# ScalarE's gate function reads PSUM itself; its clamp becomes a minimum in VectorE's product

## What is computed

```python
gu = xb @ w_gu[e] + b_gu[e]                                # rows x 2048
x_glu = jnp.minimum(gu[:, :D_FF], SWIGLU_LIMIT)            # limit 7.0
x_lin = jnp.clip(gu[:, D_FF:], -SWIGLU_LIMIT, SWIGLU_LIMIT)
act = x_glu * jax.nn.sigmoid(SWIGLU_ALPHA * x_glu) * (x_lin + 1)   # alpha 1.702
return act @ w_down[e] + b_down[e]                         # rows x 1024
```

## Time and profile before

| | |
|---|---|
| time, 3 runs | 1763.78 us median (1761.51 to 1766.02) |
| profiled execution | 1762.76 us, of which the span is 1761.0 us |
| TensorE matmul | 1653.0 us busy, 94% of the span |
| TensorE weight load | 1301.0 us, 74% |
| VectorE | 1342.6 us, 76% |
| ScalarE | 1123.3 us, 64% |
| GpSimd | 643.0 us, 37% |
| HBM read | 476.44 MB |

### The profile page before, as it was taken

How to read it: one execution, slowest core, us unless ns; L and a number is a source line. 1 busy time by engine, 2 the same in 40 slices (tenths; PEclk the granted TensorE clock), 3 DMA queues, 4 the chain that set the end, 5 groups by cost and what they waited for, 6 DMA issues and landing times.

```text
span 1761.0 us, 22444 instructions
## 1 busy us (share of the span) xinstructions
PE 1653.0 (94%) x7739; PEld 1301.0 (74%) x7739; DVE 1342.6 (76%) x1184; ACT 1123.3 (64%) x1030; POOL 643.0 (37%) x480
## 2 busy tenths in 40 slices
PE   6999999999988889999999999999999999999993
PEld 5877767889866576877777777777777777777762
DVE  4444563426343569999999999999999999999992
ACT  4134555234324245777887888888878878888882
POOL 5002231000000026346455455456456456456442
PEclk9999999999999998999999999999999999999996
DMA  9221112424441137999999999999999999999993
GB/s 317 106 95 62 60 65 74 150 79 147 164 122 48 60 130 287 392 389 395 399 401 399 402 399 397 400 399 396 400 398 398 401 403 392 402 397 395 400 377 105
DMA packets 93730, 493.11 MB, mean 280 GB/s; under 512 B 10461, under 2 KB 10530, under 8 KB 44426
## 3 DMA queue, kind: packets, MB, share of 16 engines
q1 hardware_dynamic: 82368, 459.30, 65.6%
q0 software_dynamic: 9824, 28.05, 6.0%
q10 hardware_dynamic: 1482, 5.01, 0.7%
HBM read 476.44 MB, written 20.38 MB: 282 GB/s over the span
## 4 chain that ended last, share of the span: by engine, by line
PE 40%; DVE 25%; issue 16%; DMA 9%; ACT 9%; SPq 0%; POOL 0%; DVEq 0%; ACTq 0%; POOLq 0%
DVE wlo L1548 17%; PE ps L1825 7%; PE ps L1826 7%; PE ps L1827 7%; DMA raw<-in_w_down 7%; ACT whi L1114 5%; PE ps L2278 4%; DVE glu L1588 2%; PE ps L1948 2%; PE ps L1950 2%; PE ps L1952 2%; PE ps L2248 1%; PE ps L1975 1%; DMA raw<-in_w_gu 1%; DVE lin L1590 1%
## 5 line engine op out<-in xcount | busy, mean ns | idle before, releaser
L1548 DVE TENSOR_TENSOR wlo<-raw,whi 128x2048 fp32r<-128x2048 f32 x380 | 847.3, 2283 | 33.0 <-ACT whi L1114 32.4
L1114 ACT ACTIVATE whi<-raw 128x2048 fp32r<-128x2048 f32 x380 | 716.0, 1913 | 98.8 <-DMA raw<-in_w_gu 53.3
L700 POOL TENSOR_TENSOR mark<-ident 1x1 f32<-1x1 f32 x32 | 158.6, 4956 | 340.8 <-ACT ybuf L1156 222.0
L1274 DVE TENSOR_TENSOR wlo<-raw,whi 128x2048 fp32r<-128x2048 f32 x52 | 119.3, 2317 | 147.0 <-ACT whi L846 147.0
L701 POOL DMA_INDIRECT moe_rows<-ybuf,ycur x32 | 207.4, 6482 | 6.3 <-issue 6.3
L2278 PE MATMUL ps<-whi,xhi 128*128 128x512 f32 x544 | 151.6, 401 | 3.4 <-DVE xlo L1553 2.7
L2278 PE MATMUL ps<-wlo,xhi 128*128 128x512 f32 x544 | 146.5, 391 | 0.0
L2278 PE MATMUL ps<-whi,xlo 128*128 128x512 f32 x544 | 146.5, 391 | 0.0
L846 ACT ACTIVATE whi<-raw 128x2048 fp32r<-128x2048 f32 x52 | 98.1, 1917 | 71.7 <-DVE branch L1425 30.2
L2224 PE MATMUL ps<-whi,xhl 128*128 128x512 f32 x480 | 132.4, 397 | 9.3 <-DVE xhl L1558 9.2
L2224 PE MATMUL ps<-wlo,xhl 128*128 128x512 f32 x480 | 128.6, 390 | 0.0
(11 more groups left out here) (383 smaller groups left out, 3044.3 us busy)
## 6 DMA issues: line engine op xcount, KB each, us to landing
raw<-in_w_gu SPq DMA_DIRECT2D x256, 1024.0 KB, 9.9
raw<-in_w_down SPq DMA_DIRECT2D x128, 1024.0 KB, 8.3
raw<-in_w_in SPq DMA_DIRECT2D x14, 1024.0 KB, 10.0
raw<-in_w_gate SPq DMA_DIRECT2D x8, 1024.0 KB, 5.0
raw<-in_w_xkv SPq DMA_DIRECT2D x8, 1024.0 KB, 5.0
raw<-in_w_attn_up SPq DMA_DIRECT2D x4, 1024.0 KB, 4.8
raw<-in_w_out SPq DMA_DIRECT2D x4, 1024.0 KB, 5.2
raw<-in_w_xq SPq DMA_DIRECT2D x4, 1024.0 KB, 6.8
```

The lines of the kernel that those rows point to most:

```text
L700: g.tensor_tensor(mark[:, 0:1], ident[0:1, 0:1], ident[0:1, 1:2], ALU.add)
L1114: s.activation(his[m % DEPTH], raws[m % RAWS], ACT.Copy).then_inc(hi_done, 1)
L1274: v_.tensor_tensor(wlo[:, u % RING, :], raw[:, u % RING, :], whi[:, u % RING, :].bitcast(F32), ALU.subtract).then_inc(lo_done, 1)
L1548: v_.tensor_tensor(los[m % DEPTH], raws[m % RAWS], his[m % DEPTH].bitcast(F32), ALU.subtract).then_inc(lo_done, 1)
```

## The change

The `min` at 7 in front of the gate function goes (VectorE, L1588, one instruction an expert, 32 in all). ScalarE reads PSUM banks 0 and 1 itself and waits for TensorE's `unit_used` (or, for a light expert, `gu_shifted`) in place of `glu_ready`. The gate function rises beyond 0, so the clamp is taken behind it: VectorE's product becomes `hid = min(sig, GELU_LIMIT) * lin`, with the function's value at 7. The `+ 1` of the linear half moves into its bias (one more VectorE instruction on `braw`, once), and its clip goes from [-7, 7] to [-6, 8]. TensorE's bias product, which opens the banks anew, now waits for `sig_ready` as well.

```diff
+GELU_LIMIT = LIMIT / (1.0 + math.exp(-ALPHA * LIMIT))
...
-        glu = at("glu", 108, [CAP, D])
-        sig = glu
+        sig = at("sig", 108, [CAP, D])
...
-            def gate(i1, n=CAP):
-
-                act.wait_ge(glu_ready, i1)
-                s.activation(sig[0:n, :], glu[0:n, :], ACT.Gelu_apprx_sigmoid).then_inc(sig_ready, 1)
+            def gate(i1, used_value, n=CAP):
+
+                act.wait_ge(unit_used, used_value)
+                gate_rows(i1, n)
+
+            def gate_light(i1, lights):
+
+                act.wait_ge(gu_shifted, lights)
+                gate_rows(i1, SLOTS_L)
+
+            def gate_rows(i1, n):
+                s.activation(in_turn(sig[0:n, :]), every_second(ps[0:n, 0:2, :]), ACT.Gelu_apprx_sigmoid
+                             ).then_inc(sig_ready, 1)
...
             dve.wait_ge(braw_in, 96)
+            link(v_.tensor_scalar(braw[:, D:2 * D], braw[:, D:2 * D], 1.0, None, ALU.add))
             link(v_.tensor_copy(btmp[:, :], braw[:, :]))
...
             def gate_rows(i1, n, between=None):
-                v_.tensor_scalar(in_turn(glu[0:n, :]), every_second(ps[0:n, 0:2, :]), LIMIT, None, ALU.min
-                                 ).then_inc(glu_ready, 1)
-                v_.tensor_scalar(in_turn(lin[0:n, :]), every_second(ps[0:n, 2:4, :]), LIMIT, -LIMIT, ALU.min,
+                v_.tensor_scalar(in_turn(lin[0:n, :]), every_second(ps[0:n, 2:4, :]), LIMIT + 1.0, 1.0 - LIMIT, ALU.min,
                                  ALU.max).then_inc(gu_read, 1)
                 if between is not None:
                     between()
                 dve.wait_ge(gu_read, i1)
                 dve.wait_ge(sig_ready, i1)
-                v_.scalar_tensor_tensor(out=hid[0:n, :], in0=lin[0:n, :], scalar=1.0, in1=sig[0:n, :], op0=ALU.add,
+                v_.scalar_tensor_tensor(out=hid[0:n, :], in0=sig[0:n, :], scalar=GELU_LIMIT, in1=lin[0:n, :], op0=ALU.min,
                                         op1=ALU.mult).then_inc(hid_ready, 1)
...
# TensorE, ahead of the bias product, in gate_up_light and in gate_up
                 pe.wait_ge(gu_read, free)
+                pe.wait_ge(sig_ready, free)
```

More of the change, by code:

```diff
@@ L422, in build @@
             sem(n) for n in ("sel_gu_ready", "sel_dn_ready", "gu_biased", "dn_biased"))
-        glu_ready, gu_read, sig_ready, t_ready, hid_ready, a_turned, a_hi, a_ready = (
-            sem(n) for n in ("glu_ready", "gu_read", "sig_ready", "t_ready", "hid_ready", "a_turned",
+        gu_read, sig_ready, t_ready, hid_ready, a_turned, a_hi, a_ready = (
+            sem(n) for n in ("gu_read", "sig_ready", "t_ready", "hid_ready", "a_turned",
                              "a_hi", "a_ready"))
@@ L453, in moe_landed, with every_second, in_turn @@
             return 16 * (dense_loads + m // RAWS + 1)
+        def every_second(banks):
+            return banks.rearrange("p b n -> p (b n)").rearrange("p (j q k) -> p j k q", j=4, k=2)
+        def in_turn(rows):
+            return rows.rearrange("p (j k q) -> p j k q", j=4, k=2)
         @block.sync
@@ L1176, in _ @@
                     x_part(2)
-                    gate(1)
+                    gate(1, U + 8)
                 hi(j, moe_landed(j), U + j - DEPTH + 1)
@@ L1187, in heavy_after_heavy @@
                     hi_unit(i, j)
-                gate(i + 1)
+                gate(i + 1, 12 * i + (MAIN + 8))
                 next_part(i + 2)
@@ L1202, in light_turn @@
                     hi_unit(i, j)
-                gate(i + 1, SLOTS_L)
+                gate_light(i + 1, lights)
                 x_part(i + 2)
@@ L1240, in _ @@
                         hi(j, 32 * n + moe_landed(12 * E + j), 12 * n + (TAIL + 12 * E + j - DEPTH + 1))
-                    gate(n + (E + 1))
+                    gate(n + (E + 1), 12 * n + (TAIL + 12 * E + 8))
                     x_part(n + (E + 2))
```

## The result

| | median | runs | ratio to before |
|---|---|---|---|
| before | 1764.9 us | 1761.5 to 1766.3 (4) | |
| after | 1868.5 us | 1867.9 to 1869.1 (4) | 1.059 [1.0577, 1.0603] |

The change costs 103.6 us. The profiled execution of the changed kernel took 1867.95 us, its span 1866.2. The granted clock of TensorE had a mean of 0.948 in it (0.979 before). One execution of a later experiment (e8) took 2794 us at a mean granted clock of 0.556 and is left out everywhere.

The account below looks back on a forecast made before the run. The DMA engines were taken to bound the repeated part. Start 0.2, repeated part 4.0 and tail 2.3 us summed to 6.5 us saved, from 1763.78 to 1757.3 us; the 8-in-10 range was 1749 to 1772.

Parts of the forecast that it names:

- What bounds the kernel: Repeated pairs of turns: the DMA engines bound, by all but 0 to 0.5 us of 65.7; TensorE and VectorE next.
- VectorE's minimum, 4.0 us in the repeated part: Removing it returns only DMA idle, about 0.35 us a pair over 12.5 pairs, counted as 4.0 us (bounds 0 to 6.3).
- the DMA engines hide all: Rival, repeated part: DMA idle is uneven queues and stays, only start and tail count: 1761.3 us; chance 0.20.
- The gate function from PSUM, the product: At the gates: ScalarE's strided PSUM read takes 1.1 us (1.0 to 2.2), the product's new form 1.22; both hidden.
- ScalarE no longer waits for VectorE: At the gates: ScalarE's 67.8 us of waits go; counted at nothing, without DMA cover worth 1.0 + 0.4 us a pair.
- The biases: One more VectorE instruction on the biases, some 0.8 us, hidden by 5.7 us of cover: cost 0.
- The start: First gate: the bias product can't start before 694.4, where it started at 694.6, so it gives 0.2 us.
- The tail: Behind the last heavy gate: 1.2 us on the light expert and 1.14 at the very last gate, together 2.3.
- A place where the change could bite: GpSimd: Heavy gate: GpSimd gets its turns in VectorE's PSUM reads, and the change halves that window from 2.4 to about 1.27 us.
- starved gather: Rival, heavy gate: the selects slip behind the product, the gather lands 2.5 us late a pair: 1784 us; chance 0.15.
- L2212's wait for the select: Sign of a wrong forecast: a pair above 66 us, with TensorE's L2212 waiting for GpSimd's select.

Follow-up runs that it names:

- e8: The changed kernel with a dead PSUM-reading VectorE minimum ahead of the linear half's clip, and ScalarE's gate function made to wait for it: 1767.5 us, ratio 1.0021.
- e5: The changed kernel with GpSimd's two copies (sel_gu_l, sel_dn) done ahead of the gather, not behind the scatter: 1770.0 us, ratio 1.005.
- e7: The kernel before with GpSimd's two copies (sel_gu_l, sel_dn) done ahead of the gather, nothing else: 1762.9 us, ratio 0.999.
- e1: The changed kernel with a dead VectorE minimum that reads PSUM, ahead of the linear half's clip at each gate: 1798.5 us, ratio 1.019.
- e6: The kernel before, minimum kept, with the one in the bias row, clip at -6 and 8, product as minimum times linear half: 1763.2 us, ratio 0.9996.
- e9: The changed kernel with a dead VectorE row maximum over SBUF (one operand) ahead of the linear half's clip: 1798.3 us, ratio 1.0197.
- e2: The changed kernel with a dead VectorE addition of two SBUF tensors ahead of the linear half's clip: 1896.7 us, ratio 1.074.

## Why the prediction was wrong

**What bounds the kernel** was right. e5 shows it: with VectorE 2.5 us lighter a pair, the DMA engines stay at 397 to 400 GB/s, and its heavy gates stand 66.05 us apart (1223.87 and 1289.92), no less than the 65.7 of the earlier trace rows.

**VectorE's minimum, 4.0 us in the repeated part:** nothing came back, not the 0.35 us a pair. e5 was 7 us slower than e7. Its profile shows one wait for the gather (6.0 us), but that execution was only 1.7 us slower than the profiled one of e7, so the 7 us are not accounted for. In the pairs my rival "the DMA engines hide all" is what holds once GpSimd is out of the way; its time, 1761.3, was not reached.

**The gate function from PSUM, the product:** right. The function took 1.00 us on 96 rows (predicted 1.1), the product 1.22, and VectorE waited for the function once, 0.9 us, at the first gate. **ScalarE no longer waits for VectorE:** I counted this at nothing because landings covered it. Where VectorE has its two reads of PSUM (e1 against e8) it costs 31 us, through the gather; that is a second term that I had wrong. In e5 it is at most part of the 7 us. **The biases:** right, by e6. **The start:** the bias product L2273 began at 694.06, behind ScalarE's function, which I had seen as the limit; its fellow before began at 693.92, so my "started at 694.6" was misread and the gain of 0.2 us is none. **The tail:** in e5 1765.8 - 1688.2 = 77.6 us pass from the last heavy gate to the end, against 1761.0 - 1681.8 = 79.2 before: 1.6 us, where I had 2.3.

**The step that failed is "A place where the change could bite: GpSimd", in its judgement.** I read the halved window in the rows and gave it a rival of its own, "starved gather", with 0.15. Its mechanism was right down to "the scatter just ends, the selects slip behind the product". Two things in it were wrong.

- *The argument against it.* "VectorE gets gaps of some 0.3 us in just that chain, and the scatter goes through ahead of the gate." In the changed kernel VectorE was busy for 24.00 of 24.00 us around the marker's wait (columns as in the earlier trace rows):

```profile
1241.00:1265.00 24.00, 24.00 (x118) 19.88 (x117) 24.00 (x12) 18.67 (x13) 23.10 (x1) 1.00 1.01 412
```

  Units that land at the DMA engines' pace only make gaps where VectorE is ahead of them. In this window it was not. What counts is whether an open window is left when the copies' turn comes.

- *The price: who waits for it.* I followed the gather, the last in GpSimd's line, and found 2.1 us a pair. The copy `sel_gu_l` stands two places ahead of it, and TensorE needs it at once, to open the sums of the light expert, right behind the gate. That is 7.8 us a pair, 13 times, 101 us of waiting, and with the lower clock behind it and the old small waits gone a pair of 73.4 us (heavy gates at 825.78 and, thirteen pairs later, 1779.36) instead of 65.7: 7.6 us a pair against the 2.1 I had. My last paragraph names L2212's wait for the select as a sign of this, but no sum was made of it.

**What stays open.** At the heavy gate the marker stays out over nine boundaries between two `lo` and the copy over three; alone each was let in at the first. Yet in the changed kernel itself, 10 to 25 us earlier, the other marker and another copy were let in:

```profile
1211.44 6.69 DVE L1564 TENSOR_TENSOR wlo<-raw,whi 128x2048 fp32r<-128x2048 f32 x3 [7.30 <-ACT whi L1120]
1216.27 1.92 POOL L706 TENSOR_TENSOR mark<-ident 1x1 f32<-1x1 f32 x1 [9.57 <-ACT ybuf L1179]
1218.05 0.95 DVE L1579 TENSOR_TENSOR alo<-ps,ahi 128x768 fp32r<-128x768 f32 x1
...
1228.23 4.49 DVE L1564 TENSOR_TENSOR wlo<-raw,whi 128x2048 fp32r<-128x2048 f32 x2 [4.83 <-ACT whi L1120]
1228.86 1.70 POOL L701 COPY ycur<-slots 96x2 int32 x1
```

The marker ends at 1218.19, as L1579 (PSUM and SBUF operands) has begun, and `ycur` at 1230.56, at the boundary between the two `lo`. In e1 three copies in a row came in at one boundary after the other within five `lo` without a gap (from 1228.82; the copies' rows begin at 1232.38, 1233.46 and 1235.61 and end at 1233.43, 1235.66 and 1237.85). So it is not the whole kernel as such that keeps GpSimd out. Nor is it the form alone: from 760 to 1760 us a waiting marker was let in at L1579 in 14 of 14 cases and at L1584, which has the same kinds of operands, in none of 14, where in the kernel before its twin L1568 let it in in 14 of 14. The rule of the Trainium skill named above does not predict this. Issue form, waits, loop, ScalarE, loads, buffers, GpSimd's own DMAs and TensorE were tried alone, and none of them kept a copy or the marker out for longer than one `lo`. That the copies' lost window makes the loss is shown by e5, e1, e9 and e2; why it stays closed for so long is not. No version beat the kernel before: the best with the change's saving, e5, is 0.5% slower.

## What to carry to other kernels

Before you take away an instruction of an engine that can keep another one out, list what else happens only while it runs: here the minimum was the window in which GpSimd did two small copies. Follow each operation that could be kept out to its first user, not the last of the row only; the earliest user sets the price. And if small work on GpSimd feeds TensorE, do it well before it is needed, where the order costs nothing (e7), so that no window decides.

## What the hardware showed that I had not expected

- A window is lost by half a microsecond: the scatter's issue ended at 1266.86, the product had begun at 1266.36, and the copy behind it was through only at 1277.10.
- One added VectorE instruction of 1.2 us with one operand made the changed kernel 70 us faster (e1, e9); one with two SBUF operands made it 28 us slower (e2).
- GpSimd's addition of one number can be shown as busy for 23.35 us: a waiting instruction counts as busy, so the busy time of GpSimd (768.1 us) says little of its work.
- TensorE's granted clock fell to 0.93 and 0.94 in pairs in which it had idled for 7.8 us, a mean between its levels of 1.2 and 2.4 GHz (0.5 and 1.00), and was 1.00 in both windows of e5. Even in the changed kernel the stretch just ahead of the heavy gate (1241 to 1265) has 1.00.
